# Recurrent stage of a three-layer mixer kernel: one weight split moved behind the recurrence, a half tile's products moved into the stage's head, copies of transposes ahead of other copies, GpSimd's masks held back

## What is computed

```python
q_a, k_a, v_a, z_a, b_a, a_a, q_b, k_b, v_b, z_b = split(rms_norm(x, w_norm) @ w_in)
o_a = gated_delta_rule_chunked(q_a, k_a, v_a, g, beta)   # 4 heads of 128, chunks of 64
o_b = diff_attention(q_b, k_b, v_b, lam)                 # 4 heads
out = x + concat([rms_norm(o_a) * silu(z_a), rms_norm(o_b) * (1 - lam_init) * silu(z_b)]) @ w_out

# inside gated_delta_rule_chunked, for each head and chunk:
lower = strict_lower((k * beta) @ k.T * decay)
u, w  = solve(I + lower, [v * beta, k * beta * exp(g)])  # unit triangular, 64 x 64
v_new = u - w @ state                                    # from here on one chunk after the other
o     = (q * exp(g)) @ state + (tril(q @ k.T) * decay) @ v_new
state = state * exp(g_last) + (k * exp(g_last - g)).T @ v_new
```

## Time and profile before

| | us |
|---|---|
| median of 3 runs | 1765.62 (1765.24 to 1768.19) |
| the profiled execution: its own time | 1768.61 |
| the profiled execution: span, first to last instruction | 1765.6 |
| PE busy | 1709.1 |
| DVE busy | 890.6 |
| ACT busy | 630.6 |
| POOL busy | 138.5 |

### The profile page before, as it was taken

One profiled execution on the slowest core, in us unless ns is written; L12 is line 12 of the kernel. 1 busy time (PEld: TensorE's weight loads), 2 busy tenths in 40 slices (PEclk: granted clock), 3 DMA queues, 4 the chain that ended last, 5 costly groups with the idle time before them and its releaser, 6 DMA issues.

```text
span 1765.6 us, 27912 instructions
## 1 busy us (share of the span) xinstructions
PE 1709.1 (97%) x11765; PEld 1479.9 (84%) x11765; DVE 890.6 (50%) x1156; ACT 630.6 (36%) x968; POOL 138.5 (8%) x114
## 2 busy tenths in 40 slices
PE   7999998999999999999999999999999999877998
PEld 6997777799999999999887888888877887566886
DVE  5533546474343433665566434343566468546544
ACT  4523434424132323321233223232335356553213
POOL 1000000050000000320022000000141000002100
PEclk9998999999999999999999999999999999897959
DMA  5230001023332223232223232322354662001101
GB/s 183 72 90 14 7 1 49 26 73 96 96 96 93 81 89 95 95 96 82 89 92 96 95 96 96 95 95 95 115 84 84 75 91 53 1 17 42 49 1 48
DMA packets 135633, 129.84 MB, mean 74 GB/s; under 512 B 17645, under 2 KB 131428, under 8 KB 135540
## 3 DMA queue, kind: packets, MB, share of 16 engines
q1 hardware_dynamic: 135338, 128.44, 26.3%
q10 hardware_dynamic: 202, 0.06, 0.0%
HBM read 126.39 MB, written 2.10 MB: 73 GB/s over the span
## 4 chain that ended last, share of the span: by engine, by line
PE 91%; DVE 4%; ACT 3%; issue 1%; SPq 1%; POOL 0%; DMA 0%; ACTq 0%; DVEq 0%; POOLq 0%
PE ps L455 69%; PE ps L884 3%; PE ps L2152 2%; PE ps L781 2%; PE ps L764 1%; PE ps L1119 1%; PE ps L1925 1%; PE ps L2305 1%; PE ps L1184 1%; PE ps L2281 1%; PE ps L2312 1%; PE ps L2270 1%; PE ps L789 1%; PE ps L2279 0%; PE ps L2302 0%
## 5 line engine op out<-in xcount | busy, mean ns | idle before, releaser
L430 ACT ACTIVATE w_hi<-raw 128x1024 fp32r<-128x1024 f32 (+1 forms) x227 | 239.4, 1055 | 811.7 <-PE ps L455 788.6
L455 PE MATMUL ps<-x_hi,w_hi 128*128 128x258 f32 (+4 forms) x1640 | 450.7, 327 | 3.7 <-DVE x_lo L475 2.8
L455 PE MATMUL ps<-x_lo,w_hi 128*128 128x258 f32 (+4 forms) x1640 | 444.4, 323 | 0.0
L455 PE MATMUL ps<-x_hi,w_lo 128*128 128x258 f32 (+4 forms) x1640 | 443.5, 323 | 0.0
L437 DVE TENSOR_TENSOR w_lo<-raw,w_hi 128x1024 fp32r<-128x1024 f32 (+1 forms) x227 | 296.2, 1305 | 108.0 <-ACT w_hi L430 107.9
L455 PEld LDWEIGHTS ps<-x_hi,w_hi 128*128 128x128 f32 (+2 forms) x1640 | 273.4, 188 | 34.7 <-issue 3.8
L455 PEld LDWEIGHTS ps<-x_lo,w_hi 128*128 128x128 f32 (+2 forms) x1640 | 272.4, 188 | 28.1 <-issue 2.4
L455 PEld LDWEIGHTS ps<-x_hi,w_lo 128*128 128x128 f32 (+2 forms) x1640 | 272.2, 188 | 25.7
L455 PE MATMUL ps<-a_hi,w_hi 128*128 128x258 f32 (+1 forms) x960 | 255.0, 320 | 0.3 <-DVE a_lo L983 0.3
L455 PE MATMUL ps<-a_hi,w_lo 128*128 128x258 f32 (+1 forms) x960 | 255.1, 320 | 0.0
L455 PE MATMUL ps<-a_lo,w_hi 128*128 128x258 f32 (+1 forms) x960 | 254.8, 320 | 0.0
(11 more groups left out here) (421 smaller groups left out, 1885.1 us busy)
## 6 DMA issues: line engine op xcount, KB each, us to landing
raw<-in_w_mlp_up SPq DMA_DIRECT2D x32, 1024.0 KB, 5.3
raw<-in_w_mlp_down SPq DMA_DIRECT2D x32, 1024.0 KB, 5.1
raw<-in_w_in SPq DMA_DIRECT2D x16, 1024.0 KB, 8.9
raw<-in_w_in_conv SPq DMA_DIRECT2D x12, 1024.0 KB, 5.1
raw<-in_w_in_attn SPq DMA_DIRECT2D x8, 1024.0 KB, 5.1
raw<-in_w_out_attn SPq DMA_DIRECT2D x4, 1024.0 KB, 5.2
raw<-in_w_out_conv SPq DMA_DIRECT2D x4, 1024.0 KB, 5.1
raw<-in_w_out SPq DMA_DIRECT2D x4, 1024.0 KB, 5.3
```

Source lines behind the costliest of these rows:

```text
L430: act.activation(split_tile(w_hi, t), raw_tile(t), ACT.Copy).then_inc(w_hi_ok, 1)
L455: ins = pe.matmul(pair_of_banks[t % 2][0:m, b, 0:c], w[:, k, :], x[:, k, x0:x0 + c], start=(k == order[0] and n == 0), stop=(k == order[-1 ...
```

## The change

- The row tables move into slot 0 of w_hi and w_lo, so that tile T_OUT2 (slot 1) can be split while they are in use.
- Tile T_OUT2 is split earlier: on ACT behind the last a_hi of the attention part, on DVE behind the X1 scaling.
- Half tile 0 goes to bank 7 and is issued in two pieces within the transposes of TT, ahead of heads 0 and 2; DVE adds it ahead of TT of head 3. Half tile 1 waits for that addition. The transposes of head 3, which use the same bank, wait for it too.
- ACT copies the transposes (TM) ahead of the egl copies.
- GpSimd's level-1 masks wait for all four TT, and not each for that of its own head.
- In the levels ten pieces are left: one in level 1, three in each of levels 2 to 4, none in level 5. DVE's additions and splits move with them; the split of T_OUT2 + 3 goes into level 5, between the TT updates of heads 0 and 1.
- DVE's split of T_OUT2 + 4 goes behind the recurrence.

```diff
@@ -1670,9 +1670,10 @@
         EG, NEG_G, BETA, NEG_BEG, SOFT, MASK, G, KD = (row(i) for i in range(8))
         gcol = at("gdn_cols", x_off + 32768, [P, 4, 4, GH])
 
-        row_hi_lo = [at(f"rows_{n}", off["w_hi"] + 2048 * i, [P, SEQ], F32R) for i, n in enumerate(("decay", "beta", "exp"))]
-        G_R, BETA_R, EG_R = row_hi_lo
-        row_cols = at("row_cols", off["w_lo"], [P, SEQ])
+        other = 4096 * (1 - T_OUT2 % 2)
+        G_R, BETA_R, EG_R = [at(f"rows_{n}", off[w] + other + o, [P, SEQ], F32R)
+                             for n, w, o in (("decay", "w_hi", 0), ("beta", "w_hi", 2048), ("exp", "w_lo", 0))]
+        row_cols = at("row_cols", off["w_lo"] + other + 2048, [P, SEQ])
 
         def rows_pool(pool):
 
@@ -2130,7 +2131,7 @@
 
         def half_tile_banks(q):
 
-            return ps[:, 6 + q % 2, :] if q < KC else ps[:, 2 * ((T_OUT2 + q // 2) % 2) + q % 2, :]
+            return ps[:, 7 if q == 0 else 6 + q % 2, :] if q < KC else ps[:, 2 * ((T_OUT2 + q // 2) % 2) + q % 2, :]
 
         def half_tile_pe(pe, q, part=None):
 
@@ -2139,6 +2140,8 @@
             rows = (4, 5, 6, 7) if q < KC else OUT_ORDER
             if part in (None, 0):
                 pe.wait_ge(w_lo_ok, t + 1)
+                if q == 1:
+                    gd.wait(pe, "half_in", 1)
                 if q >= 2 and q not in (8, 9, 10, 11):
                     if x == 0:
                         gd.wait(pe, "half_in", q // 2)
@@ -2237,7 +2240,13 @@
                 gd.wait(pe, "lt", h + 1)
                 pe.matmul(A_bank(h), hsel[0:64, h, :], EG_R[0:64, :], start=True, stop=True).then_inc(gd.s["row_pe"], 1)
             for h in range(GH):
+                if h % 2 == 0:
+                    gd.wait(pe, "lt", 2 * GH)
+                    dz.wait(pe, "out_lo", 4)
+                    half_tile_pe(pe, 0, h // 2)
                 gd.wait(pe, "tt", h + 1)
+                if h == 3:
+                    gd.wait(pe, "half_in", 1)
                 for j in range(4):
                     ins = pe.transpose(pblk(B_bank(h), j), blk(TT, h, j), tab["ident"][:, :])
                 ins.then_inc(gd.s["t_pe"], 1)
@@ -2255,8 +2264,7 @@
                     ins = pe.matmul(pblk(A_bank(h), j), blk(LB, h, j), blk(TM, h, j), start=True, stop=True)
                 ins.then_inc(gd.s["y_pe"], 1)
             PAIRS = ((0, 1), (2, 3))
-            dz.wait(pe, "out_lo", 4)
-            pieces = [0]
+            pieces = [2]
             def piece():
                 half_tile_pe(pe, pieces[0] // 2, pieces[0] % 2)
                 pieces[0] += 1
@@ -2268,7 +2276,7 @@
                         gd.wait(pe, "tnew", (i - 2) * GH + h + 1)
                         gd.wait(pe, "ttnew", (i - 2) * GH + h + 1)
                     by_chunks(pair, lambda h, r, c: pe.matmul(A_bank(h)[r, c], LB[r, h, c], TM[r, h, c], start=True, stop=True), "y_pe")
-                if i > 1:
+                if 1 < i < 5:
                     piece()
                 for pair in PAIRS:
                     for h in pair:
@@ -2280,7 +2288,7 @@
                                                                   half(YY[r, h, c], b, 0), start=True, stop=True), "d_pe")
                     by_chunks(pair, lambda h, r, c: pe.matmul(A_bank(h)[r, c.start:c.start + CH // 2], YY[r, h, c], half(TT[r, h, c], b, 1),
                                                               start=True, stop=True), "dt_new_pe")
-                    if i < 5:
+                    if i < 5 and (i > 1 or pair[0]):
                         piece()
             gd.wait(pe, "half_in", 3)
             pe.wait_ge(evicted, T_OUT2 + 3)
@@ -2331,19 +2339,19 @@
                     ins = act.activation(blk(KDEC, h, j), pblk(A_bank(h), j), ACT.Copy, scale=gcolumn(kd_c, h, j))
                 ins.then_inc(gd.s["scaled"], 1)
             dif_last_act(act)
+            split_hi(act, T_OUT2)
             for h in range(GH):
                 gd.wait(act, "dt_pe", h + 1)
                 for j in range(4):
                     ins = act.activation(blk(YY, h, j), pblk(A_bank(h), j), ACT.Exp, bias=gcolumn(negG, h, j))
                 ins.then_inc(gd.s["dt"], 1)
             for h in range(GH):
+                gd.wait(act, "t_pe", h + 1)
+                act.activation(TM[:, h, :], B_bank(h), ACT.Copy).then_inc(gd.s["t"], 1)
+            for h in range(GH):
                 gd.wait(act, "row_pe", GH + h + 1)
                 gd.wait(act, "qg", h + 1)
                 act.activation(egl[:, h, :], A_bank(h)[:, CH - 1::CH], ACT.Copy).then_inc(gd.s["egl"], 1)
-            for h in range(GH):
-                gd.wait(act, "t_pe", h + 1)
-                act.activation(TM[:, h, :], B_bank(h), ACT.Copy).then_inc(gd.s["t"], 1)
-            split_hi(act, T_OUT2)
             split_hi(act, T_OUT2 + 1)
             for i in range(1, 6):
                 if i in (3, 4):
@@ -2387,7 +2395,7 @@
                     if i == 0:
                         gd.wait(pool, "lt", GH + h + 1)
                     elif i == 1:
-                        gd.wait(pool, "tt", h + 1)
+                        gd.wait(pool, "tt", GH)
                     else:
                         gd.wait(pool, "y_pe", GH * (i - 2) + h + 1)
                     pool.tensor_tensor(blocks(LB[:, h, :]), blocks(LT[:, h, :]), every_block(gmask[:, 1 + i, :]), ALU.mult).then_inc(gd.s["lvl"], 1)
@@ -2402,6 +2410,7 @@
             for n, h in enumerate((0, 2, 3, 1)):
                 gd.wait(dve, "turned_v", n + 1)
                 dve.tensor_tensor(blocks(X1[:, h, :]), blocks(B_bank(h)), columns(beta_c, h), ALU.mult).then_inc(gd.s["scaled_v"], 1)
+            split_lo(dve, T_OUT2)
             for n, h in enumerate((0, 2, 3, 1)):
                 gd.wait(dve, "kq", n + 1)
                 gd.wait(dve, "dt", h + 1)
@@ -2420,6 +2429,8 @@
                     gd.wait(dve, "lt", GH + h + 1)
                     dve.tensor_tensor(blocks(LB[:, h, :]), blocks(LT[:, h, :]), every_block(gmask[:, 1, :]), ALU.mult).then_inc(gd.s["lvl_dve"], 1)
                     gd.wait(dve, "lvl_dve", h - GH // 2 + 1)
+                if h == 3:
+                    half_tile_dve(dve, 0)
                 dve.tensor_tensor(blocks(TT[:, h, :]), every_block(tab["ident"][:, :]), blocks(LB[:, h, :]), ALU.subtract).then_inc(gd.s["tt"], 1)
             def mask(i, h):
 
@@ -2433,16 +2444,15 @@
                 dve.tensor_tensor(qk_a(h), qk_a(h), A_bank(h), ALU.mult).then_inc(gd.s["qg"], 1)
                 if 1 <= h <= 2:
                     mask(1, h + 1)
-            split_lo(dve, T_OUT2)
             for i in range(1, 6):
                 if 2 <= i:
-                    half_tile_dve(dve, (0, 2, 3, 5)[i - 2])
+                    half_tile_dve(dve, (1, 2, 4, 5)[i - 2])
                 for h in range(GH):
                     u = (i - 1) * GH + h
-                    if h == 2 and i in (2, 4):
-                        half_tile_dve(dve, i - 1 if i == 2 else 4)
-                    if h == 2 and i in (1, 3, 4):
-                        split_lo(dve, T_OUT2 + (1, 0, 2, 3)[i - 1])
+                    if h == 2 and i == 3:
+                        half_tile_dve(dve, 3)
+                    if h == 2 and i == 1 or h == 1 and i in (3, 5):
+                        split_lo(dve, T_OUT2 + (i + 1) // 2)
                     if i == 1:
                         gd.wait(dve, "t", h + 1)
                     if i < 5:
@@ -2454,7 +2464,6 @@
                     dve.tensor_tensor(odd, odd, halves_of(A_bank(h), LEVELS[i]), ALU.subtract).then_inc(gd.s["ttnew"], 1)
                     if i < 5 and h >= GH // 2:
                         mask(i + 1, h)
-            split_lo(dve, T_OUT2 + 4)
             for turn in TURNS:
                 for h, n in turn:
                     r = slice(CH * (n % 2), CH * (n % 2) + CH)
@@ -2477,6 +2486,7 @@
                         gd.wait(dve, "state", nth(h, n - 1, hi=NCH - 1))
                         ins = dve.scalar_tensor_tensor(ST[:, h, :], ST[:, h, :], egl[:, h, n:n + 1], B_bank(h)[:, P:2 * P], ALU.mult, ALU.add)
                     ins.then_inc(gd.s["state"], 1)
+            split_lo(dve, T_OUT2 + 4)
             def split(n):
                 h = OUT_ORDER[n]
                 gd.wait(dve, "o_hi", n + 1)
```

## The result

| | before | changed |
|---|---|---|
| median, us | 1765.86 (1765.24 to 1768.19, 4 runs) | 1739.67 (1737.05 to 1744.78, 4 runs) |
| ratio to before | | 0.9853 (95% interval 0.9829 to 0.9877) |
| profiled execution: span, us | 1765.6 | 1743.0 |

A second set of runs of the changed kernel, on another chip, gave 1741.88, ratio 0.9884 (0.9859 to 0.991).

What follows compares the result with a forecast made beforehand. PE, busy 97% of the span, was taken as the bound. Gains of 2.5 + 0.7 + 1.4 + 3.0 + 1.5 = 9.1 us brought the median of 1765.62 to 1756.5 us, range 1749.0 to 1762.5.

Steps and rivals of the forecast that it cites:

- the term for the granted clock at the start of the recurrence: Recurrence: without the pause, two short first turns at the high clock save 1.5 us, bounds 0 to 3.
- rival 2: Recurrence: the clock stays high throughout, seven turns at 3.3 us instead of 4.86 give 11; 1747 us, chance 0.07.
- Early split of T_OUT2: Before the head: ACT and DVE halves of the split fit into existing waits, cost 0.
- The head: From LT to the end of level 1's first four products: gain 2.5 us, bounds -0.4 to 5.0.
- the second case drawn: Head: clock falls at the start, then comes back; TT of head 3 at 1617.7, first level-1 product at 1619.2.
- The case in which the clock stays low: Head: clock low throughout, TT of head 3 at 1618.9, first level-1 product at 1620.3, loss 0.4 us.
- Contention: Behind TT: two DVE masks blocked by GpSimd's would eat about 2 us of the 2.1 regained.
- Level 1: One piece less, PE restarts at 1630.05 and not 1630.79: gain 0.7 us, up to 0.3 less.
- rival 4: Levels: the clock doesn't come back, some 20 us more, 1778 us; chance 0.12, one third of it a short spell.
- Levels 2 to 5: One piece less in level 5: gain 1.4 us, with DVE's split there hidden; levels 2 to 4 keep three pieces each.
- Start of the recurrence: Moving DVE's split of T_OUT2+4 behind the recurrence removes PE's wait for V copies: gain 3.0 us.
- Rivals 1, 3 and 4: Low clock in whole head, 1759.4 (0.15); pause ahead of recurrence stays, 1761.1 (0.05); low clock in levels, 1778 (0.12).

Runs made afterwards that it cites:

- e2: Changed kernel with DVE's split of tile T_OUT2+4 back ahead of the recurrence: 1761.36 us, ratio 0.9981.
- e1: Kernel before with one edit, DVE's split of tile T_OUT2+4 moved behind the recurrence: 1744.94 us against 1765.26, ratio 0.9867.
- e4: Changed kernel with the split of T_OUT2+4 and two unused 128x1024 DVE subtractions in the recurrence's fifth turn: 1752.41 us, ratio 0.9922.
- e5: Changed kernel with GpSimd's level-1 masks released by each head's own TT again: 1740.07 us, beside 1739.67 of the changed kernel.
- e6: Changed kernel with ACT's egl copies ahead of the T copies again: 1745.84 us, ratio 0.9902.
- e7: Changed kernel with level 1's second piece back, level 4's middle piece out, split of T_OUT2+2 one level earlier: 1737.54 us, later 1736.90.
- e3: Kernel before with 24 unused 128x256 products on PE in the pause ahead of the recurrence: 1747.08 us, ratio 0.9892.
- e8: Changed kernel with the split of T_OUT2+4 and one unused 128x512 DVE subtraction in the recurrence's fifth turn: 1743.26 us.
- f1: e3 with 16 and with 8 of its 24 unused products: 1746.87 and 1746.92 us.
- e9: e7 plus 16 unused 128x512 products in PE's wait ahead of the transposes of V: 1737.46 us.
- e10: e9 plus six 128x512 products on PE in the wait ahead of the first half tile: 1737.69 us.

## Why the prediction was wrong

**The step that failed** is the term for the granted clock at the start of the recurrence: 1.5 us, with an upper bound of 3, where 14.8 were measured in the recurrence and 2.8 behind it. It stood on one sentence, under rival 2: "in 39 us of busy PE it never came back, so work of this kind doesn't earn it". The observation was right, the conclusion wasn't: that work doesn't raise the clock says nothing on whether it loses it. e2 shows the first (38.1 us at 0.50), e1 the second (23.4 us at 1.00), and e4 both levels in one trace. The norms behind the recurrence (2.8) stood in no term. Rival 2 (1747, chance 0.07) named the mechanism, and the range, which ended at 1749.0, left it out. It undersold it too: it took 3.3 us for a turn that the chain through DVE would bound; measured 3.1, with PE busy throughout; and it left out the norms behind the recurrence. With the recurrence as measured (14.8 for 1.5) the rival's sum would be 9.1 + 13.3 + 2.8 = 25.

The Trainium skill (TensorE: Matmul & The Clock Gate, Part 1) says that activity releases the throttle. For a PE that starts busy at 1.00 the runs agree (23.45 us); for one that starts at 0.50 they don't in general: in e2 a PE that was busy for 38.1 us stayed there.

**Point by point.**
- Early split of T_OUT2: hidden, as said. From the first decay product to the end of LT it is 16.3 us in both kernels.
- The head: 3.1 for 2.5, along the second case drawn (the clock falls at the start of the pieces and comes back). Shifted by the 1.0 of the later entry, TT of head 3 was due at 1618.7 and the first level-1 product at 1620.2; measured 1618.60 and 1620.15. But the credit was misplaced: holding the masks back gives nothing (e5), the order of ACT's copies gives it: without it the head is 5.1 us longer (e6). The case in which the clock stays low was added up wrongly: its own terms put TT of head 3 at 1619.4, not at 1618.9; it didn't come. A piece at the low clock isn't "twice" 1.59, but the 2.7 us taken for it were right: 2.69 in level 1.
- Contention: two fully blocked masks would have cost about 2 us. Measured 0.79 and 1.16 us in place of 0.68: 0.6. The Trainium skill (SBUF — State Buffer, Who interferes with whom) says that the one of two such instructions that starts later is blocked until the other ends. Here DVE's masks lost 0.11 and 0.48 us beside GpSimd's, which took 1.3 to 1.7 us each; whether they met only the end of a block or shared the port no run here shows.
- Level 1: 0.7 forecast, -1.0 measured. The wait that comes to light was 0.94, as worked out (0.9), and where the clock stayed at 1.00 the missing piece gave 0.6 (e6: 6.57 us for 7.14). The short fall of the clock was missed here: 1.6 us (8.15 for 6.57). It is rival 4's mechanism in small, and e7 takes it away.
- Levels 2 to 5: 1.4 forecast, 1.0 measured. Level 5 itself gave 1.2 (5.88 to 4.65 us). DVE's split in level 3 now stands ahead of the update of head 1 and PE waits 0.49 us for it; I had given that move no cost.
- Start of the recurrence: 3.0 and 3.0; the split is hidden behind it.
- Rivals 1, 3 and 4 didn't come: behind its first 7 us, which ran at 0.50 as before, the stage was at 1.00 but for 3 to 4 us twice, and the pause was gone.

## What to carry to other kernels

Read from the trace where PE's clock falls and what was idle just before, and price every microsecond behind that point at both levels; a pause of 3 us cost 3 us and 18 more. Where a wait can't be removed, dense products that nobody reads hold the clock, but only if the next wait is short as well. A level that some work can't raise may still be a level that it keeps: don't infer one from the other.

## What the runs showed of the hardware

- The recurrence (products with a side of 64, PE busy throughout) stays at whichever of 2.4 and 1.2 GHz it enters with: 23.4 to 23.5 us in the changed kernel, e1 and e3, 38.1 to 38.2 before and in e2.
- Ahead of or in the recurrence, idle PE of 0.57 (e8), 1.14 and 2.08 us (f1) kept the clock; 2.24 (e4) and 3.02 us (before, e2) lost it, as did 3.00 us ahead of the decay products (e9).
- Shorter waits amid thin work lost it too: 1.11 us ahead of the half tile in the head (not with e10's products in it), and in level 1 no wait over 0.94 us, with one piece in place of two. Level 1 of e6 has the same piece and wait and kept it, behind 6.5 us of PE busy without a break. So no single length of a wait decides.
